# Twelve weight units of the SSM scan split by casting and adding DMAs, the gate products on VectorE, and the scan's outputs taken in another order

## What is computed

```python
v = a * jax.nn.sigmoid(g)                       # a, g: halves of u_glu
v = causal_dwconv(v, dw_w, dw_b)                # 31 taps, 1024 channels
...
y_diag = einsum("bcgls,bcsgrp->bclgrp", cb[:, :, :, None] * decay, xs)
states = einsum("bclgn,bcgrl,bclgrp->bcgrpn", bc, decay_states, xs)
y_off  = einsum("bclgn,bcgrpn,bcgrl->bclgrp", cc, prev, exp(a_cs))
y  = y_diag + y_off + xh * d_skip
yg = y * jax.nn.silu(z)
yg = yg * rsqrt(mean(square(yg)) + RMS_EPS)     # per group
```

## Time and profile before

| | us |
|---|---|
| median of 3 runs | 2252.87 |
| lowest, highest | 2248.13, 2253.51 |
| the profiled execution, its own time | 2250.25 |
| its span in the trace | 2248.4 |
| the scan, from its first matmuls to the group sums | about 185 to 440 of the span |

### The profile page before, as it was taken

The page is one execution under the profiler, slowest core; times in us unless marked ns, Lnnn a source line. Parts: engine busy times, 40 slices in busy tenths (PEclk is TensorE's granted clock), DMA queues, the critical chain, the costliest instruction groups (busy, mean ns, idle before and its releaser), DMA issues.

```text
span 2248.4 us, 31753 instructions
## 1 busy us (share of the span) xinstructions
PE 2187.6 (97%) x12988; PEld 1915.8 (85%) x12988; DVE 1442.6 (64%) x1841; ACT 960.2 (43%) x1393; POOL 54.1 (2%) x45
## 2 busy tenths in 40 slices
PE   9999989899999999999999999999999999999997
PEld 6888777688887888888999999999999889888887
DVE  4878899899757656646676685135357658722544
ACT  5446665632524444433547543223233565322321
POOL 1000000000000000000200000000000000000001
PEclk9999999999999999999999999999999999999999
DMA  4222233222221322243211212222222112222221
GB/s 152 94 105 105 89 107 106 82 92 96 94 86 67 110 94 94 95 150 131 98 66 49 95 59 93 94 94 94 85 85 98 57 38 94 103 103 94 94 94 57
DMA packets 35696, 207.69 MB, mean 92 GB/s; under 512 B 4930, under 2 KB 6978, under 8 KB 12260
## 3 DMA queue, kind: packets, MB, share of 16 engines
q1 hardware_dynamic: 28944, 193.48, 24.2%
...
## 4 chain that ended last, share of the span: by engine, by line
PE 79%; DVE 11%; DVEq 4%; ACT 4%; issue 1%; DMA 1%; ACTq 1%; SPq 0%
PE PS L561 25%; PE PS L565 24%; PE PS L563 24%; DVE vout L2101 4%; DVEq L2094 1%; DVE wlo L1840 1%; PE PS L1079 1%; ACT whi L1184 1%; PE PS L1053 1%; DMA acs_b<-acs_rows 0%; DVE acc L1993 0%; PE PS L1069 0%; DVE res L1964 0%; ACT sc L1613 0%; PE PS L874 0%
## 5 line engine op out<-in xcount | busy, mean ns | idle before, releaser
L561 PE MATMUL PS<-ahi,whi 128*128 128x512 f32 (+2 forms) x2368 | 732.1, 344 | 12.0 <-DVE upad L2552 3.3
L563 PE MATMUL PS<-alo,whi 128*128 128x512 f32 (+2 forms) x2368 | 719.0, 339 | 0.0
L565 PE MATMUL PS<-ahi,wlo 128*128 128x512 f32 (+2 forms) x2368 | 718.6, 339 | 0.0
L1840 DVE TENSOR_TENSOR wlo<-raw,whi 128x2048 fp32r<-128x2048 f32 x172 | 393.9, 2290 | 460.7 <-ACT whi L1184 460.2
L1184 ACT ACTIVATE whi<-raw 128x2048 fp32r<-128x2048 f32 x168 | 321.7, 1915 | 662.1 <-PE PS L565 658.0
L561 PEld LDWEIGHTS PS<-ahi,whi 128*128 128x128 f32 x2368 | 414.6, 189 | 74.7 <-issue 24.8
L563 PEld LDWEIGHTS PS<-alo,whi 128*128 128x128 f32 x2368 | 413.8, 189 | 48.1 <-issue 1.4
L565 PEld LDWEIGHTS PS<-ahi,wlo 128*128 128x128 f32 x2368 | 413.3, 189 | 48.4
L561 PE MATMUL PS<-f2hi,whi 128*128 128x264 f32 (+2 forms) x800 | 214.9, 314 | 0.0
L563 PE MATMUL PS<-f2lo,whi 128*128 128x264 f32 (+2 forms) x800 | 214.9, 314 | 0.0
L565 PE MATMUL PS<-f2hi,wlo 128*128 128x264 f32 (+2 forms) x800 | 214.8, 314 | 0.0
...
## 6 DMA issues: line engine op xcount, KB each, us to landing
raw<-weights SPq DMA_DIRECT2D x180, 1024.0 KB, 4.7
...
x_in<-x_t SPq DMA_DIRECT2D x4, 512.0 KB, 6.1
...
raw<-weights SPq DMA_DIRECT2D x1, 512.0 KB, 10.7
cols<-columns ACTq DMA_DIRECT2D x1, 385.0 KB, 7.1
...
```

What stands on the lines that cost most here:

```text
L561: nc.tensor.matmul(o, wh, h, start=first, stop=False)
L563: nc.tensor.matmul(o, wh, h, start=False, stop=False)
L565: mm = nc.tensor.matmul(out[j], wl, hi[j], start=False, stop=last)
L1840: v.tensor_tensor(wlo[s][:, :], raw[s][:, :], whi[s][:, :].bitcast(F32), ALU.subtract).then_inc(lo_ready, 1)
```

## The change

1. **Twelve units by DMA.** z2 to z13 no longer go through `raw`, the rounding and the subtraction. POOL issues a DMA that casts the weights into the rounded format straight into `hi` (`cast`), ACT writes `lo` = -`hi` (`negated`), and POOL issues a second DMA of the same weights that adds them to `lo` (`added`). The units use three pairs of buffers in turn; the third, `w_raw_hi` and `w_raw_lo`, lies where the two `raw` buffers are. PE's `claim` waits for both DMAs and raises `lo_ready` itself. SP skips these loads, and z14's load waits until z12 is multiplied.
2. **Gate products.** All 16 are on DVE now (`gated`), in `y_out(j)` and at the group's end. `gate_go` is gone.
3. **DVE's order.** Outputs stand ahead of the filler; `TAPS_AT` moves most taps to the group's end, and 4 taps of the last tile leave the scan for later.
4. **ACT's order.** See below; the negation for z3 of a group stands behind heads 0 to 3, that for the next group's z0 behind head(4), and the one of glu_unit(0) no longer waits for `unit_done`. In group 3 the split for z15 stands behind head(4), the next one behind head(6), and four squares that stood ahead of head(4) stand behind head(7).

```diff
-TAPS_AT = [0, 4, 8, 10, 13, 14, 18, 26, 31]
-LAST_TAPS = 21
+TAPS_AT = [0, 4, 5, 6, 8, 10, 23, 31]
+LAST_TAPS = 17
...
+CAST0, CASTS = WORK["z_glu"].u0 + 2, 4 * GROUPS - 4
...
+            return CAST0 <= u < CAST0 + CASTS
...
+            return w3[(u - CAST0) % 3] if by_cast(u) else w2[u % 2]
...
-            for u in range(2, WORK["gate_b"].u0 + 1):
+            for u in (*range(2, CAST0), *range(CAST0 + CASTS, WORK["gate_b"].u0 + 1)):
                 sp.wait_ge(lo_ready, u - 1)
+                if u == CAST0 + CASTS:
+                    sp.wait_ge(unit_done, u - 2)
                 sp.dma_start(raw[u % 2][:, :], wstream[SOURCE[u]]).then_inc(raw_in[u % 2], 16)
...
+            def cast(u):
+                j = u - CAST0
+                if j == 0:
+                    pool.wait_ge(lo_ready, CAST0)
+                else:
+                    pool.wait_ge(unit_done, u - 2)
+                nc.gpsimd.dma_start(w3[j % 3][0][:, :], wstream[SOURCE[u]]).then_inc(cast_in[j % 3], 16)
+            def added(u):
+                j = u - CAST0
+                pool.wait_ge(hi_ready, u + 1)
+                nc.gpsimd.dma_start(w3[j % 3][1][:, :], wstream[SOURCE[u]], accum_op=ALU.add
+                                    ).then_inc(cast_in[j % 3], 16)
...
-            for k in range(XT - 1):
-                pool.wait_ge(zs_ok, k // 2 + 1)
-                pool.wait_ge(gate_go, k + 1)
-                t = xbc[:, k * T:(k + 1) * T]
-                nc.gpsimd.tensor_tensor(t, t, zs[k % GP][:, :], ALU.mult).then_inc(yg_ok, 1)
+            cast(CAST0)
+            for g in range(GROUPS - 1):
+                u = WORK["z_glu"].u0 + 4 * g
+                cast(u + 3)
+                added(u + 2)
+                added(u + 3)
+                cast(u + 4)
+                added(u + 4)
+                cast(u + 5)
+                added(u + 5)
+                if g < GROUPS - 2:
+                    cast(u + 6)
...
 def claim(stage, i, s):
+    if by_cast(stage.u0 + 2 * i + s):
+        j = stage.u0 + 2 * i + s - CAST0
+        pe.wait_ge(cast_in[j % 3], 32 * (j // 3 + 1))
+        pe.sem_inc(lo_ready, 1)
...
+def negated(u):
+    j = u - CAST0
+    act.wait_ge(cast_in[j % 3], 32 * (j // 3) + 16)
+    hi, lo = w3[j % 3]
+    nc.scalar.activation(lo[:, :], hi[:, :].bitcast(F32), ACT.Copy, scale=-1.0).then_inc(hi_ready, 1)
...
 def glu_unit(u):
-    split_next(stage, 2 * g + u // 2, u % 2)
+    if u == 0:
+        prepared(2)
+    act.wait_ge(unit_done, stage.u0 + 4 * g + u + 1)
...
 for q in range(4):
     head(q)
+if g < GROUPS - 1:
+    prepared(3)
 z_unit(1)
-split_next(stage, 2 * g, 1)
 head(4)
+prepared(4 if g < GROUPS - 1 else 3)
 head(5)
 head(6)
-split_next(stage, 2 * g + 1, 0)
+if g == GROUPS - 1:
+    prepared(4)
 head(7)
...
+    prepared(5)
     glu_unit(3)
```

`prepared(u)` is `negated` for the twelve units and the old split for the others. DVE's list of a group, as a diff:

```diff
                     mask(q)
+                y_out(0)
                 taps(0)
-                y_out(0)
-                taps(1)
+                y_out(1)
                 mask(4)
                 low_next(stage, 2 * g, 1)
+                taps(1)
                 mask(5)
                 taps(2)
-                y_out(1)
+                y_out(2)
+                mask(6)
                 taps(3)
+                mask(7)
+                low_next(stage, 2 * g + 1, 0)
+                taps(4)
                 if g == GROUPS - 1:
                     squares_added(2)
-                y_out(2)
-                mask(6)
-                taps(4)
-                mask(7)
-                low_next(stage, 2 * g + 1, 0)
-                taps(5)
                 y_out(3)
                 if g < GROUPS - 1:
-                    taps(6)
+                    taps(5)
                     low_next(stage, 2 * g + 1, 1)
-                    hold(dve, sig_ok, 2 * g + 3, "dve")
-                    drain().then_inc(gate_go, 1)
+                    gated(g * GP + GP - 1)
                     glu(1)
                     for j in range(2):
                         x_scaled(g + 1, j)
-                    taps(7)
-            last = xbc[:, (XT - 1) * T:XT * T]
-            dve.wait_ge(zs_ok, 2 * GROUPS)
-            dve.wait_ge(yg_ok, XT - 1)
+                    taps(6)
             drain()
-            v.tensor_tensor(last, last, zs[GP - 1][:, :], ALU.mult).then_inc(yg_ok, 1)
+            gated(XT - 1)
+            long_taps([KD - 1], TAPS_AT[5], TAPS_AT[5] + 3)
             squares_added(GROUPS - 1)
```

More of the change, by code:

```diff
@@ L303, in tile, with by_cast, weights, raw_loads @@
                 return self.psum((slot * 2 + m) * self.parts)
+        def by_cast(u):
+            return CAST0 <= u < CAST0 + CASTS
+        def weights(u):
+            return w3[(u - CAST0) % 3] if by_cast(u) else w2[u % 2]
+        def raw_loads(u):
+            return 16 * (u // 2 + 1 - (CASTS // 2 if u >= CAST0 + CASTS else 0))
         every = Span(True)
@@ L358, in build @@
         hi_ready, lo_ready = sem("whi_ready"), sem("wlo_ready")
+        cast_in = [sem(f"cast_in{j}") for j in range(3)]
         unit_done, tile0_done = sem("unit_done"), sem("tile0_done")
@@ L568, in claim, with tile @@
             def claim(stage, i, s):
-                hold(pe, lo_ready, stage.u0 + s + 1 + 2 * i, "pe")
+                if by_cast(stage.u0 + 2 * i + s):
+                    j = stage.u0 + 2 * i + s - CAST0
+                    pe.wait_ge(cast_in[j % 3], 32 * (j // 3 + 1))
+                    pe.sem_inc(lo_ready, 1)
+                else:
+                    hold(pe, lo_ready, stage.u0 + s + 1 + 2 * i, "pe")
                 hold(pe, psum_free[stage.slot(s)], stage.used(i, s), "pe")
-            def tile(stage, hi, lo, width, parts, s, m, ks, base=None, stride=None, first=0):
+            def tile(stage, hi, lo, width, parts, s, m, ks, base=None, stride=None, first=0, i=0):
                 slot = stage.slot(s)
@@ L2316, in _ @@
             low_at(stage_b.u0 + 2)
[L2317 removed]
+            long_taps([KD - 1], TAPS_AT[5] + 3, LAST_TAPS)
             dve.wait_ge(ss_std, 1)
```

42 lines of the change are left out of this document (27 added, 15 removed).

## The result

| | us |
|---|---|
| before, median of 12 runs | 2249.45 (2244.75 to 2253.51) |
| changed, median of 12 runs | 2258.2 (2255.17 to 2261.2) |
| ratio | 1.0040, 95% interval 1.0031 to 1.0049 |
| profiled execution, before and changed | 2250.25 and 2256.57 |
| span, before and changed | 2248.4 and 2254.8 |

The changed kernel is 0.4% slower. The forecast was 2240, 12.9 us faster on the profiled execution; the profiled execution became 6.3 us slower. The measured median lies inside the stated range of 2233 to 2268, but the sign is wrong, and the error is 19 us in the sum.

A forecast was written before the change was run, and what follows sets the result against it. TensorE, busy 97% of the span, was taken as the bound: 30.8 us winnable less 17.9 of costs gives 12.9 won, 2250.25 to 2237.4 profiled, a 2240 us median. The 8-in-10 range was 2233 to 2268.

The forecast's parts named there:

- stalls and slow matmuls that can go: In the scan, PE's waits for masks and states (23.2 us) plus slower matmuls after stalls (7.6): 30.8 us winnable.
- stalls at pair(2), groups 0 to 2: PE waiting for masks at pair(2): 4.1 us in group 0, nothing in groups 1 and 2.
- stalls at pair(3), groups 0 to 2: All old mask stalls at pair(3) go; two hand-overs at 0.3 us remain, 0.6 us.
- waits for `xds`: 21 taps instead of 13 between y_out(3) and the end of `xds`: PE waits 1.7 us three times, 5.1.
- group 3: z15's split between head(4) and head(5) costs 1.7 at pair(2), 0.4 at pair(3); the end 2.5: 4.6 us.
- slow matmuls behind stalls: On PE in the scan, one stall above 2.5 us is followed by slower matmuls, 1.5 us.
- behind the scan: Four taps moved after the scan, where DVE feeds PE too: 2 us, between 0 and 3.3.
- S: Time from POOL's issue of z3's addition until the next group's z0 cast has landed, taken as 9.6 us.
- rival (a): An addition reads target and weights, 2.88 us more: S = 12.5, W = 5.7, 1.4 us lost, 2254 us; chance 0.22.
- W: ACT's wait behind head(4) for the next group's z0 cast: S less 6.8 us of own work, 2.8 us.
- the 3.6 us in hand: Head(5)'s margin in groups 1 and 2 from earlier heads; only W - 3.6 would show, nothing at W = 2.8.
- Rival (b): POOL's casting and adding transfers as slow as the slowest here: S = 14.2 or 17.8, 2263 or 2284 us; chance 0.24.

## Why the prediction failed, step by step

The profiled execution is 6.3 us slower where 12.9 us faster was forecast. By the terms of the sum:

| term | forecast | measured |
|---|---|---|
| stalls and slow matmuls that can go | 30.8 | 30.8 |
| stalls at pair(2), groups 0 to 2 | 4.1 | 4.43 + 6.12 + 2.74 = 13.3 |
| stalls at pair(3), groups 0 to 2 | 0.6 | 1.65 + 2.10 + 1.29 = 5.0 |
| waits for `xds` | 5.1 | 1.37 + 2.19 + 2.20 = 5.8 |
| group 3 | 4.6 | 1.28 + 0.28 + 1.87 + 0.32 = 3.8 |
| slow matmuls behind stalls | 1.5 | 9.4 |
| behind the scan | 2 | 1.3 |
| ahead of the scan | 0 | -1.3 |
| sum of costs | 17.9 | 37.2 |

The slow matmuls are the scan's 6.4 us, plus 23.2 + 7.6, less the waits of 27.8. The 1.3 us ahead of the scan can't be put down to the change: over all the kernels run here the scan's `b_transposes` start between 185.3 and 186.8, and with the change's casts alone (no second transfer) at 186.7. The first step held, and so did the three that concern VectorE: the old stalls at pair(3) disappeared, 21 taps ahead of `xds` cost what the subtraction of rows gave, and group 3 came out within a microsecond. The claim for both DMAs cost PE nothing, as said. Two steps failed: the price of an addition in S, and the broadcasts, which had no term at all. The slow matmuls follow from these: they were priced for one stall and came behind four waits.

**The price of an addition.** S was put together from a plain load's 4.7 us, its 2.88 of transfer for the cast behind, and 2 us of issuing. Issuing was overpriced: a cast alone lands only 0.5 us after a plain load would. (The Trainium skill's page "DMA: Bandwidth & Descriptors", section "Specifications", puts the first byte 0.4 us later from POOL; the trace agrees, though its 0.5 us hold the conversion too.) The cast behind was about right, 2.5 to 4 us after the addition. The addition's landing was the error, 7.9 us for 4.7. The forecast named a second read as rival (a), gave it S = 12.5 and 0.22, and set against it that the engines had room. Room in the mean is no argument for one chain: what counts is how long one transfer takes. Rival (a) was right that an addition costs more than a cast (whether by a second read stays open), its signs were the ones seen (additions landing clearly later than casts, stalls at pair(2) in groups 0 to 2), and its S close to the 10.5, 12.0 and 10.9 measured. A second term of W was off by less: ACT's own work in between is 6.0 us (215.98 - 4.53 - 205.46), not 6.8, since head(4) ends 2.4 us after its start (2.9 is the distance between the starts of two heads) and the addition is issued 0.3 us after the negation's end.

**The broadcasts.** The forecast cited their 6.4 us beside a load as evidence for the queue, and did not price them. But with POOL's queue busy 39.2% of the scan, ScalarE's waits for them went from 10.2 us in the scan before (the longest is in the earlier trace rows) to 26.0. They took the early start away that groups 1 and 2 were to have (the 3.6 us in hand): head(2) of group 1 waited 4.49 us at 264.28, head(3) began at 267.14 where it had begun at 265.47. So W came in full, and pair(2) of group 1 stalled for 6.12 us where nothing was expected. And head(7)'s broadcast stalled pair(3). This is why rival (a)'s 1.4 us lost was 6.3 in the profiled execution: about 5 us that no case had, and that with an S below its 12.5. Rival (b), a loss above 0.3%, gave the right sign by the wrong mechanism: casts are nearly as prompt as plain loads, 5.2 us.

That both steps count is shown by runs: the cast moved ahead won 8.9 us, the addition held back 10.6, both 22.7. With both, the kernel is 14.0 us faster than before, about the gain that the forecast had claimed for the change as it stood; that the two numbers are near is chance, since this is another kernel.
